# The end of a two-block transformer kernel: last tile's upper columns added in two parts, its last squares summed on VectorE, tile zero's rows scaled on ScalarE, the last gain product moved

## The reference, cut to what matters

```
def _rmsnorm(x, g):
    x32 = x.astype(jnp.float32)
    y = x32 * lax.rsqrt(jnp.mean(x32 * x32, axis=-1, keepdims=True) + EPS)
    return y.astype(x.dtype) * g

        hf = _rmsnorm(h, norm_ffn_g[l]) @ w_ff1[l]
        h = h + jnp.square(jax.nn.relu(hf)) @ w_ff2[l]
    return _rmsnorm(h, norm_final_g)
```

## Time and profile before

| What | us |
|---|---|
| median of 3 runs (lowest, highest) | 929.91 (929.64, 929.93) |
| the profiled execution's own time | 931.16 |
| its span, first to last instruction | 929.4 |
| PE busy in the span | 918.4 (99%) |
| DVE, ACT, POOL busy | 684.9, 523.9, 15.2 |

### The profile page before, as it was taken

How to read it: one execution, slowest core, us unless ns; L and a number is a source line. 1 busy time by engine, 2 the same in 40 slices (tenths; PEclk the granted TensorE clock), 3 DMA queues, 4 the chain that set the end, 5 groups by cost and what they waited for, 6 DMA issues and landing times.

```text
span 929.4 us, 14094 instructions
## 1 busy us (share of the span) xinstructions
PE 918.4 (99%) x5341; PEld 787.6 (85%) x5341; DVE 684.9 (74%) x1205; ACT 523.9 (56%) x899; POOL 15.2 (2%) x20
## 2 busy tenths in 40 slices
PE   8999999999999999999999999999999999999997
PEld 6899887788888888888899988888788888888886
DVE  5779976378776666678688989998786676666665
ACT  6656677745654544456544436654946664445443
POOL 0300000000000000000000000000000000000000
PEclk9999999999999999999999999999999999999999
DMA  9845454655565555554655844555475256655551
GB/s 334 307 146 159 137 150 127 237 200 186 166 207 196 193 193 189 193 190 147 206 173 151 235 134 154 172 175 178 138 236 176 93 163 219 217 189 182 181 182 46
DMA packets 89458, 168.54 MB, mean 181 GB/s; under 512 B 7536, under 2 KB 11952, under 8 KB 89136
## 3 DMA queue, kind: packets, MB, share of 16 engines
q1 hardware_dynamic: 89024, 167.13, 55.5%
q10 hardware_dynamic: 368, 0.52, 0.2%
HBM read 164.77 MB, written 1.05 MB: 178 GB/s over the span
## 4 chain that ended last, share of the span: by engine, by line
PE 94%; DVE 3%; issue 1%; DMA 1%; ACT 1%; SPq 0%; POOLq 0%; POOL 0%; DVEq 0%
PE pb L429 92%; PE pb L433 2%; DVE YC L1987 1%; DVE wlo L1527 1%; DMA raw<-in_w_in 1%; ACT whi L976 0%; DVE DG L1966 0%; DVE ST L1677 0%; DVE XS L2261 0%; ACT S L1461 0%; DVE SM L1672 0%; SPq L367 0%; DVE X L2254 0%; DVE ST L2209 0%; ACT SM L976 0%
## 5 line engine op out<-in xcount | busy, mean ns | idle before, releaser
L1527 DVE TENSOR_TENSOR wlo<-raw,whi 128x1024 fp32r<-128x1024 f32 (+2 forms) x300 | 356.0, 1212 | 118.0 <-ACT whi L976 117.4
L976 ACT ACTIVATE whi<-raw 128x1024 fp32r<-128x1024 f32 (+2 forms) x302 | 308.7, 1044 | 134.3 <-PE pb L429 122.2
L429 PE MATMUL pb<-XT,whi 128*128 128x256 f32 (+2 forms) x1424 | 311.1, 334 | 0.8 <-issue 0.8
L429 PEld LDWEIGHTS pb<-XT,whi 128*128 128x128 f32 (+1 forms) x1424 | 234.9, 190 | 23.7 <-issue 4.0
L429 PE MATMUL pb<-whi,ZO 128*128 128x512 f32 (+1 forms) x808 | 252.4, 389 | 0.0
L429 PE MATMUL pb<-XT,wlo 128*128 128x256 f32 (+1 forms) x1032 | 205.5, 282 | 0.0
L429 PE MATMUL pb<-whi,XT 128*128 128x512 f32 (+1 forms) x544 | 176.3, 395 | 2.3 <-ACT whi L976 2.3
L429 PEld LDWEIGHTS pb<-whi,ZO 128*128 128x128 f32 x808 | 151.3, 188 | 31.6 <-DVE wlo L1527 1.1
L429 PEld LDWEIGHTS pb<-XT,wlo 128*128 128x128 f32 (+1 forms) x1032 | 166.8, 190 | 9.6
L429 PE MATMUL pb<-wlo,ZO 128*128 128x512 f32 (+1 forms) x404 | 156.6, 388 | 0.0
L429 PEld LDWEIGHTS pb<-whi,XT 128*128 128x128 f32 x544 | 101.8, 189 | 23.9 <-ACT whi L976 2.8
(11 more groups left out here) (238 smaller groups left out, 593.2 us busy)
## 6 DMA issues: line engine op xcount, KB each, us to landing
raw<-in_w_in SPq DMA_DIRECT2D x107, 512.0 KB, 3.8
raw<-in_w_ff SPq DMA_DIRECT2D x64, 512.0 KB, 4.7
raw<-in_w_up SPq DMA_DIRECT2D x32, 512.0 KB, 4.5
raw<-in_w_down SPq DMA_DIRECT2D x32, 512.0 KB, 5.1
raw<-in_w_branch_b SPq DMA_DIRECT2D x8, 512.0 KB, 4.8
raw<-in_w_out SPq DMA_DIRECT2D x8, 512.0 KB, 4.7
raw<-in_wx_kv SPq DMA_DIRECT2D x8, 512.0 KB, 5.2
raw<-in_w_attn_out SPq DMA_DIRECT2D x8, 512.0 KB, 3.4
```

Of the source, the lines that this page charges most:

```text
L429: return e.matmul(o, l, r, start=start, stop=stop, skip_group_check=True)
L976: return e.activation(o, i, ACT.Copy, scale=scale)
L1527: e.tensor_tensor(wlo[u % NW][:, 0:c], raw[u % NRAW][:, 0:c], whi[u % NW][:, 0:c].bitcast(F32), ALU.subtract).then_inc(lo, 1)
```

## The change

Five edits, all in the last 17 us of the program:

- VectorE adds bank 7's upper 256 columns (chunks 0 to 6) to X before the pieces of chunk 7 are added, in one instruction of its own (new L2253), once chunk 6 is done. `end_add` 4 takes 256 columns in place of 512. Before TensorE writes bank 7 for chunk 7 it waits for that instruction (semaphore `end_upper`), and so does `end_add` 5.
- The squares of the last 256 columns are multiplied and summed by VectorE with a scalar_tensor_tensor that has a sum (new L2290), in place of ScalarE's second L1501.
- Tile 0's left half is scaled by ScalarE too, ahead of the right half: VectorE's 512-column L2269 is gone and ScalarE has two 512-column copies.
- Tile 1's mean is made by two VectorE instructions in a row (L2293: two of the sums and D*EPS; L2295: plus `NLAST`).
- The gain product of the last 256 columns is issued behind the mean, not ahead of it. GpSimd's loop for the last norm is written with other semaphore counts.

```diff
-END_PARTS = (((0, 1, 0, 512), (1, 1, 512, 1024)), ((0, 2, 0, 320), (1, 2, 640, 1024), (0, 3, 320, 640)))
+END_PARTS = (((1, 1, 0, 512), (1, 2, 512, 1024)), ((0, 1, 0, 320), (1, 3, 640, 1024), (0, 2, 320, 640)))
...
                 for t, i, c0, c1 in ((0, 0, 0, 512), (0, 1, 0, 512), (1, 0, 0, 512), (1, 1, 0, 256), (1, 1, 256, 512)):
+                    if (t, i, c0) == (1, 1, 0):
+                        e.wait_ge(end_upper, 1)
...
-                (i, n, a, b), = (p for p in END_PARTS[t] if p[0] == 1)
-                copy(XS[:, t * D + a:t * D + b], XS[:, t * D + a:t * D + b], NR[N_END][t]).then_inc(end_out[1], 1)
+                for i, n, a, b in END_PARTS[t]:
+                    if i == 1:
+                        copy(XS[:, t * D + a:t * D + b], XS[:, t * D + a:t * D + b], NR[N_END][t]).then_inc(end_out[1], 1)
...
-            for j, acc in ((0, NS[N_END][1, 1]), (1, NLAST)):
-                a = D + 512 + 256 * j
-                e.wait_ge(end_x, 4 + j)
-                e.activation(MSQ[:, 512 + 256 * j:768 + 256 * j], X[:, a:a + 256], ACT.Square,
-                             accum_out=acc).then_inc(squares, 1)
+            e.wait_ge(end_x, 4)
+            e.activation(MSQ[:, 512:768], X[:, D + 512:D + 768], ACT.Square,
+                         accum_out=NS[N_END][1, 1]).then_inc(squares, 1)
...
+            e.wait_ge(unit_done, first["f2_dn6_1"] + 2)
+            e.scalar_tensor_tensor(out=X[:, D + 768:2 * D], in0=PB[7][:, 256:512], scalar=NR[N_FFN][1],
+                                   in1=X[:, D + 768:2 * D], op0=ALU.mult, op1=ALU.add).then_inc(end_upper, 1)
...
-            end_out_rows(0)
             end_add(3, 1, 0, 512, 5)
             step(end_gain(3, 1, 0, 512))
-            end_add(4, 1, 512, 1024, 7)
+            end_add(4, 1, 512, 768, 7)
             step(end_gain(4, 1, 512, 768))
+            e.wait_ge(end_upper, 1)
             end_add(5, 1, 768, 1024, 0)
+            e.wait_ge(end_x, 5)
+            e.scalar_tensor_tensor(out=MSQ[:, 768:1024], in0=X[:, D + 768:2 * D], scalar=1.0, in1=X[:, D + 768:2 * D],
+                                   op0=ALU.mult, op1=ALU.mult, accum_out=NLAST).then_inc(summed, 1)
             e.wait_ge(squares, 4 * N_END + 4)
-            step(e.tensor_tensor(NSUM[N_END][1], NS[N_END][1, 0], NS[N_END][1, 1], ALU.add))
+            e.tensor_scalar(NSUM[N_END][1], NS[N_END][1, 0], NS[N_END][1, 1], D * EPS, ALU.add, ALU.add).then_inc(summed, 1)
+            e.wait_ge(summed, 2 * POW[N_END] + 3)
+            e.tensor_scalar(NMEAN[N_END][1], NLAST, NSUM[N_END][1], None, ALU.add).then_inc(summed, 1)
             end_gain(5, 1, 768, 1024).then_inc(end_g, 1)
-            after_step()
-            e.wait_ge(squares, 4 * N_END + 5)
-            e.tensor_scalar(NMEAN[N_END][1], NSUM[N_END][1], NLAST, D * EPS, ALU.add, ALU.add).then_inc(summed, 1)
             end_out_rows(1)
```

More of the change, by code:

```diff
@@ L294, in build @@
         bg_in, gf_in, stored = sem("gate_bias_landed"), sem("final_gain_landed"), sem("stored")
-        end_tile, end_x, end_g = sem("end_tile"), sem("end_x"), sem("end_gained")
+        end_tile, end_x, end_g, end_upper = sem("end_tile"), sem("end_x"), sem("end_gained"), sem("end_upper_columns_added")
         end_out = [sem("end_left"), sem("end_right")]
@@ L417, in sync_program @@
                 for i, n, a, b in END_PARTS[t]:
-                    if (i, n) != (1, 2):
+                    if (i, n) != (1, 3):
                         e.wait_ge(end_out[i], n)
@@ L1485, in end_scale @@
                 e.wait_ge(factor, 2 * POW[N_END] + t + 1)
-                (i, n, a, b), = (p for p in END_PARTS[t] if p[0] == 1)
-                copy(XS[:, t * D + a:t * D + b], XS[:, t * D + a:t * D + b], NR[N_END][t]).then_inc(end_out[1], 1)
+                for i, n, a, b in END_PARTS[t]:
+                    if i == 1:
+                        copy(XS[:, t * D + a:t * D + b], XS[:, t * D + a:t * D + b], NR[N_END][t]).then_inc(end_out[1], 1)
                 if t == 1:
-                    e.wait_ge(end_out[1], 2)
+                    _, n, a, b = END_PARTS[1][1]
+                    e.wait_ge(end_out[1], n)
                     e.dma_start(outv[:, 1, a:b], XS[:, D + a:D + b]).then_inc(stored, 16)
@@ L2315, in pool_program @@
             power(KRS, KSA, 30, 1).then_inc(kc_rs, 1)
-            for n in (N_MEM, N_MIX, N_XA, N_END):
+            for n in (N_MEM, N_MIX, N_XA):
                 norm(n)
+            for t, n in ((0, 1), (1, 4)):
+                e.wait_ge(summed, 2 * POW[N_END] + n)
+                power(NR[N_END][t], NMEAN[N_END][t], P, 1).then_inc(factor, 1)
         block = ctx.enter_context(nc.Block())
```

## The result

| What | before | changed |
|---|---|---|
| median of 21 runs, us | 929.77 (928.66 to 931.23) | 930.93 (929.93 to 932.39) |
| ratio, 95% interval | | 1.0016 (1.0010 to 1.0021) |
| profiled execution's span | 929.4 | 928.7 |
| TensorE's last matmul ends | 923.67 | 922.09 |
| from there to the end of GpSimd's power | 2.06 | 2.18 |

A forecast was written before the change was run, and what follows sets the result against it. TensorE was taken to bound the kernel, leaving only the tail behind its last matmul. Terms -0.03 + 0.03 + 0.12 = +0.12 us on 929.91 gave 930.03, said as 930.0; 8-in-10 range 929.4 to 930.8.

The forecast's parts named there:

- SP's first two transfers: Output transfers issued by SP: leaving at 921.66 and 922.3, landing before 925, ahead of SP's next issue at 926.18; cost nothing.
- effects elsewhere in the program that no row names: Leftover case, such as code lying some bytes further on: up to 1 us either way, chance 0.06.
- the hold: GpSimd's last power: VectorE's gain product, started first, locks the shared port and delays the power's end, +0.12 us.
- The fifth add: VectorE's add of the last missing piece of X: starts 0.05 earlier at best, limited by TensorE; -0.03 us counted.
- From the fifth add's end to the mean's end: Last squares and sums moved to VectorE: 0.89 us against 0.86, accumulator read taken as 0.10; +0.03 us.
- The new add: VectorE's separate add of bank 7's upper columns: takes 0.48 in idle time, ends near 913.2; costs nothing.
- TensorE's new wait: TensorE's wait for the new add before its fourth piece at 920.64: met 7.4 us ahead, costs nothing.
- ScalarE's second copy: ScalarE's added 512-column copy, 0.72 us: sums ready by 923.5, needed at 924.6; costs nothing.
- The third add: VectorE's add behind TensorE's third piece: starts at 920.84, 0.42 us earlier, directly released by TensorE.
- The late wait of TensorE: Rival: the new add ends after 920.64, TensorE pauses and its clock falls; +2.9 us, 932.8; chance 0.02.
- The small gain: Rival: free accumulator, power starting before the product, or early square's sum; -0.15 us, 929.8, up to -0.7; chance 0.27.
- the change frees what cannot be used: Rival: 0.6 us saved on VectorE gives nothing since TensorE's end stands; 929.9 alone, within the forecast's range.

## Why the prediction was wrong

**The size failed on one step, at which nothing was counted.** Behind the power's end the forecast took the kernel's last stretch as it was: it weighed SP's first two transfers ("they land before 925 ... nothing") and then ended its sum. The stretch grew from 3.62 to 4.46, +0.84: a fetch of VectorE's code met the last output transfers. The prediction bounded every case by the 2.1 us of tail "that the edits touch on the path", and the loss lay behind these. Code that is longer was named only among the "effects elsewhere in the program that no row names", with 0.06 and up to 1 us. The row that would have named it was on the page: 23 q14 packets of kind instruction, each 8 KB. Where the last of them lies, behind the span's end, could have been read from the DMA view. How likely this case was, five kernels can't tell: of the numbers of instructions tried in the kernel before, 0 and 1 more cost nothing, 2 cost 0.95 us, 6 some 0.3 (within the interval), 20 nothing.

**The path to the power: +0.12 forecast, +0.12 measured, the hold rightly and the rest by luck.** Two steps were off by 0.06 and 0.05 in opposite ways. By its steps:

- The fifth add: 0.05 earlier was forecast at best, -0.03 counted. It starts 0.12 after TensorE's end, where it started 0.09 after it: +0.03. The limit was named rightly (TensorE, idle time 0.57 before the add). What was missed is the second semaphore on that add, 0.08 us, which two runs without it show.
- From the fifth add's end to the mean's end: +0.03 forecast; it is 923.53 - 922.69 = 0.84 against 0.86, so -0.02. The accumulator read is 0.08 long but runs beside the small sum, which starts at the same time, and so costs nothing; the last small sum took 0.21, the upper end.
- The hold of GpSimd's power: +0.12 forecast, +0.11 measured (0.66 against 0.55), with the power's end 0.41 behind the product's end, as computed; and 0.55 again when the product starts second. The Trainium skill (SBUF — State Buffer, § SBUF: two separate sides) states that whichever of the two starts first has the shared ports for its whole instruction, and that the other is blocked fully. The trace agrees for GpSimd, whose power is held to the product's end and then takes 0.41. It does not agree for VectorE: the product that started 0.02 behind the power ran beside it and took 0.44 in place of 0.41. There the measurement decides.
- The new add, TensorE's new wait and ScalarE's second copy cost nothing, as forecast. The third add starts 0.04 behind TensorE's piece, counted as in the forecast (919.22 to 919.26).

**The rivals.** The late wait of TensorE did not come: its matmuls have no gap. The small gain did not come either. That the change frees what cannot be used is true, and more so than said: the early add is superfluous altogether.

**What remains.** 0.12 and 0.84 make 0.96 us, against the 0.98 between the medians of 929.71 and 930.69 in the section on the result: nothing of size is missing from the tail. The medians of all runs are 1.16 apart, and the interval of the ratio, put in us, goes from 0.93 to 1.95. Whether the 0.2 between 0.96 and 1.16 is chance stays open; no run was made on it.

## What to carry to other kernels

Instructions added on VectorE, in idle time and far ahead, moved the place of its last code fetch: look in the DMA view for the instruction packets of the last microseconds, and count a fetch as a transfer that can delay the one the program ends with. Compare a version with some spare instructions in idle time before an edit of a short tail is blamed or praised for tenths of a microsecond. Before an engine is relieved, ask what the first instruction behind the relief waits for: here 0.6 us freed on VectorE gave nothing, since TensorE's end stood 0.05 behind it.

## What was not expected of the hardware

- One 8 KB code fetch among output packets of 1.3 and 1.5 KB delays the end by 0.84 and 0.86 us (two kernels), over twice what the packet itself is busy (0.5% of 16 engines over 4.4 us, 0.35 us). The rest lies in seven data packets beside it that take longer than their medians; why they do was not settled.
- Passing to a new block of code may hold VectorE by 0.35 to 0.4 us (two places, above; a third does not show it).
- A second semaphore on one VectorE instruction costs 0.08 us on the path (lag 0.12 against 0.04 behind TensorE's end). The run with one wait less shows it alone; the run without the early add has the same 0.04.
- VectorE's accumulator read is 0.08 us and hidden beside the next instruction, where ScalarE's is 0.19 and adds 0.10.
